# Input projection of a hybrid encoder layer: splitting the next weight tile before, instead of after, the next block's activations

## The reference

```python
xn = rmsnorm(xp, g_attn_pre[l])
h = xn @ w_in                                   # (tokens, 1024) @ (1024, 1184)
cq, ckv, kpe, qs, ks, vs = jnp.split(h, IN_SPLIT_POINTS, axis=-1)
q = (rmsnorm(cq, g_q) @ w_uq).reshape(b, t, MLA_HEADS, MLA_NOPE + MLA_ROPE)
ckv_n = rmsnorm(ckv, g_kv);  kpe = rope(kpe, pos)
```

## Time and profile before

| | us |
|---|---|
| median of three runs | 2798.33 |
| lowest and highest of them | 2790.84, 2800.78 |
| the profiled execution | 2798.33 |
| its span, first to last instruction | 2796.5 |
| TensorE busy in the span | 2672.3 (96%) |
| VectorE, ScalarE, GpSimd busy | 1900.8, 1425.9, 481.4 |

### The profile page before, as it was taken

How to read it: one execution, slowest core, us unless ns; L and a number is a source line. 1 busy time by engine, 2 the same in 40 slices (tenths; PEclk the granted TensorE clock), 3 DMA queues, 4 the chain that set the end, 5 groups by cost and what they waited for, 6 DMA issues and landing times.

```text
span 2796.5 us, 44995 instructions
## 1 busy us (share of the span) xinstructions
PE 2672.3 (96%) x13603; PEld 2439.9 (87%) x13603; DVE 1900.8 (68%) x2793; ACT 1425.9 (51%) x3042; POOL 481.4 (17%) x400
## 2 busy tenths in 40 slices
PE   8999978999999987999999999999999999999997
PEld 7999844677777776999999999999999999999997
DVE  6877677788788737777478754687546875568743
ACT  5443367576667744644355443454435544355532
POOL 1111041244334433000200022000220002200001
PEclk9999999899999999999999999999999999999999
DMA  7666655444555242343334433244333443334432
GB/s 220 215 216 230 218 146 154 81 76 84 88 87 86 71 140 76 113 135 122 114 99 138 163 117 109 96 140 161 116 113 102 136 163 117 104 103 131 127 119 88
DMA packets 181776, 357.73 MB, mean 128 GB/s; under 512 B 50693, under 2 KB 119781, under 8 KB 180325
## 3 DMA queue, kind: packets, MB, share of 16 engines
q1 hardware_dynamic: 181636, 356.00, 42.5%
HBM read 301.28 MB, written 55.43 MB: 128 GB/s over the span
## 4 chain that ended last, share of the span: by engine, by line
PE 56%; DVE 3%; ACT 1%; issue 1%; DMA 1%; POOL 1%; SPq 0%; ACTq 0%; DVEq 0%; POOLq 0%
PE mf_acc L2191 56%; DVE mix_w_lo L2352 1%; DMA room<-in_w_up 1%; ACT mix_w_hi L2245 1%; POOL mf_ss L2147 1%; PE mf_st L2229 0%; DMA room<-in_w_out 0%; DVE mf_x L2370 0%; DVE mf_x L2375 0%; DVE mf_rstd L2387 0%; DVE mf_xn L2403 0%; DVE mf_y L2457 0%; DVE mf_y L2465 0%; ACT mf_sq L2268 0%; ACT mf_sq L2302 0%
## 5 line engine op out<-in xcount | busy, mean ns | idle before, releaser
L2352 DVE TENSOR_TENSOR mix_w_lo<-room,mix_w_hi 128x1024 fp32r<-128x1024 f32 (+1 forms) x338 | 471.2, 1394 | 559.9 <-ACT mix_w_hi L2245 559.2
L2191 PE MATMUL mf_acc<-mix_a_hi,mix_w_hi 128*128 128x424 f32 (+1 forms) x2016 | 724.0, 359 | 30.1 <-ACTq L2248 12.2
L2191 PE MATMUL mf_acc<-mix_a_lo,mix_w_hi 128*128 128x424 f32 (+1 forms) x2016 | 717.3, 356 | 0.0
L2191 PE MATMUL mf_acc<-mix_a_hi,mix_w_lo 128*128 128x424 f32 (+1 forms) x2016 | 717.1, 356 | 0.0
L2245 ACT ACTIVATE mix_w_hi<-room 128x1024 fp32r<-128x1024 f32 (+1 forms) x338 | 383.1, 1133 | 520.8 <-PE mf_acc L2191 486.7
L2191 PEld LDWEIGHTS mf_acc<-mix_a_hi,mix_w_hi 128*128 128x128 f32 x2016 | 382.0, 189 | 45.7 <-issue 16.7
L2191 PEld LDWEIGHTS mf_acc<-mix_a_hi,mix_w_lo 128*128 128x128 f32 x2016 | 382.5, 190 | 10.5
L2191 PEld LDWEIGHTS mf_acc<-mix_a_lo,mix_w_hi 128*128 128x128 f32 x2016 | 382.2, 190 | 8.7 <-issue 0.7
L2191 PE MATMUL mf_acc<-mf_h_hi,mix_w_hi 128*128 128x424 f32 (+1 forms) x944 | 338.9, 359 | 6.9 <-DVE mix_w_lo L2352 3.9
L2191 PE MATMUL mf_acc<-mf_h_hi,mix_w_lo 128*128 128x424 f32 (+1 forms) x944 | 335.0, 355 | 0.0
L2191 PE MATMUL mf_acc<-mf_h_lo,mix_w_hi 128*128 128x424 f32 (+1 forms) x944 | 334.6, 354 | 0.0
(11 more groups left out here) (204 smaller groups left out, 4099.5 us busy)
## 6 DMA issues: line engine op xcount, KB each, us to landing
room<-in_w_up SPq DMA_DIRECT2D x220, 512.0 KB, 3.5
room<-in_w_down SPq DMA_DIRECT2D x80, 704.0 KB, 4.1
pi_w_raw<-in_w_in SPq DMA_DIRECT2D x49, 512.0 KB, 6.1
room<-in_w_out SPq DMA_DIRECT2D x40, 512.0 KB, 3.6
la_rec_all<-inv_scr SPq DMA_DIRECT2D x32, 256.0 KB
ahead_k<-kn_scr SPq DMA_DIRECT2D x28, 280.0 KB, 5.4
ahead_q<-qn_scr SPq DMA_DIRECT2D x28, 264.0 KB, 5.1
room<-in_x SPq DMA_DIRECT2D x4, 1696.0 KB, 12.0
```

Source lines behind the costliest of these rows:

```text
L2191: mm = pe.matmul(acc[:, t_bank[0], 0:n], w[:, g, k], x[:, k, 0:n], start=(first and k == 0 and m == 0), stop=(last and k == count - 1 and ...
L2352: dve.tensor_tensor(w_lo[:, g, 0:count], w_raw[:, g, 0:count], w_hi[:, g, 0:count].bitcast(F32), ALU.subtract).then_inc(w_split, 1)
```

## The change

At steps j = 4 to 9 ScalarE and VectorE used to make the x tile of the next block first and split the weight tile after it. At j = 2 and 3 it was the other way round. The change makes j = 4 to 9 like j = 2 and 3: weight tile first, x tile after it. No instruction is added or removed, and SyncE, GpSimd and TensorE keep their order.

```diff
@@ ScalarE @@
-                    if 4 <= j <= KD + 1 and not last:
-                        x_tile(b + 1, j - 2, 1 - par)
                     if t + SLOTS - 1 < TILES and t > 0:
                         w_hi_of(t + SLOTS - 1)
-                    if 2 <= j < 4 and not last:
+                    if 2 <= j <= KD + 1 and not last:
                         x_tile(b + 1, j - 2, 1 - par)
```

## The result

The changed kernel takes 2812.44 us (median of five runs, 2810.11 to 2814.5), the kernel before 2797.61 us beside it: a ratio of 1.0056 with a 95% interval of 1.004 to 1.0072. Measured a second time as e1_again it took 2808.3 us against 2798.66, 1.0041 (1.0025 to 1.0057). So it is slower by about 0.4 to 0.6%, some 10 to 15 us. I forecast 2805 with a range up to 2812, which the first median passes by 0.4 us, and gave slower by over 0.5% a chance of 0.09.

What follows compares the result with a forecast made beforehand. TensorE, busy 96% of the span, was taken as the bound; 4.7 us of boundary delay at tile 41 plus 1.7 for one clock fall made 6.4 us on 2798.33, forecast 2805 us, range 2795 to 2812.

Steps and rivals of the forecast that it cites:

- End of block 0: First block boundary: the x tile starts one weight tile later, so TensorE, already waiting for it, slips 1.1 us.
- End of block 1: Second boundary: weight tile 22 split 1.3 us late, TensorE waits 1.5 us for x tile 7, sum slips 2.6.
- the ring: Chain of VectorE, ScalarE and SyncE beside TensorE's own, product to store to x load; weight tiles 1.3 us late at boundaries.
- End of block 2: Third boundary: weight tile 32 split at 207.4, x tile 7 done at 210.3, sum at 210.85, slip 4.4 us.
- End of block 3: Fourth boundary: weight tile 42 at 272.2, sum at 275.65, slip 5.95; tile 41 at 278.65, +4.7 us.
- accumulator wait: TensorE's 1.06 us wait at 273.94, before tile 41, for a freed accumulator; forecast to vanish.
- Clock: TensorE's clock after new boundary waits of 1.5 to 1.9 us: one fall taken, +1.7 us, bounds 0 and 10.
- Inside a block: Steps j = 4 to 8: -0.6 us at j = 4 in blocks 2 and 3, +0.15 in block 1, otherwise nothing.
- Rival A: Block boundaries: TensorE drags the ring along, lateness repeats in full; +9.0 us, 2809 with one clock fall; chance 0.16.
- Rival B: Block boundaries: nothing moves, the last x tile turns out early enough; 2798 us; chance 0.10.
- C (long falls): Three boundary waits: each brings a clock fall, mean price 5.0 us, giving 2818 us; chance 0.09.
- D (faster): Projection: earlier weight splits bring the ring ahead, waits of 1.0 and 1.3 us go; 2796 us; chance 0.08.

Runs made afterwards that it cites:

- e3_last_only: Kernel before with only step j = 9 swapped, j = 4 to 8 as before: 2812.17 us, ratio 1.0044 (1.0029 to 1.0059).
- e4_add_waits: Changed kernel with GpSimd's addition of a block's last squares waiting until VectorE has made the last x tile: 2809.87 us, ratio 1.0037 to the kernel before.
- e7_tensor_late: Kernel before with eight extra sums on TensorE ahead of the sum at the start of block 2, delaying TensorE alone: 2802.0 us, one run.
- e2_last_old: Changed kernel with step j = 9 put back as before, so only j = 4 to 8 swapped: 2801.03 us, ratio 1.0008 (0.9999 to 1.0017).

## Why the prediction was wrong

What makes the loss, its place and its sign were right. How the loss is carried from one boundary to the next was not, and so the size was too small, 6.4 us for what is 9.8 us at tile 41 (both with one clock fall) and 9.6 and 14.8 us in the two measurements. Step by step:

- *End of block 0*, forecast 1.1: measured 2.4. VectorE's chain was already 1.3 us late when it reached the swapped pair (79.67 for 78.38). Of it, 0.5 is the store of `q_scr` (product at 68.16 for 67.62, which scatters), and 0.7 a latent's scaling that took 1.34 us for 0.66, beside an addition on GpSimd. The second part goes with the swaps of j = 4 to 8: the scaling took 0.81 to 1.55 us in the five traces that have them, 0.66 in the other five. The swap of the last step then cost the forecast 1.1.
- *End of block 1*, forecast ring 1.3 late and x tile 0.65 us long: measured 2.9 and 1.47. The slip at the sum is 5.1 for 2.6: my 2.6, plus 1.6 of a later ring, plus 0.8 of the x tile, make 5.0.
- *End of block 2*, forecast weight tile 32 at 207.4, slip 4.4. Measured 210.91 and 8.9. Again 4.4 + 3.5 + 0.8 = 8.7.
- *End of block 3*, forecast weight tile 42 at 272.2, slip 5.95. Measured 276.26 and 11.0, with 5.95 + 4.1 + 0.8 = 10.8; and tile 41 at 283.70, not 278.65. The accumulator wait went as forecast.
- *Clock*, forecast one fall at 1.7 us: there was one, behind the sum at 148.25, where the granted clock is 0.57 over 4 us (below), 1.7 us by the slip of later rows. It fell by luck on the forecast number: e1_again had one fall at another boundary, e3_last_only and e4_add_waits three.
- *Inside a block*, forecast -0.6 at j = 4 and nothing at j = 6 to 8: the idle 0.67 us of the earlier trace rows shrank to 0.25, but what was gained was lost at once, as the x tile behind it now takes 1.50 us:

```profile
179.24 1.23 DVE L544 TENSOR_TENSOR pi_w_lo<-pi_w_raw,pi_w_hi 128x1024 fp32r<-128x1024 f32 x1 [0.25 <-ACT pi_w_hi L412]
180.39 1.50 DVE L549 SCALAR_TENSOR_TENSOR pi_x_lo<-room,pi_gx,pi_x_hi 128x424 fp32r<-128x424 f32 x1
```

The step that failed is the lateness of the ring, which I took as 1.3 us at every boundary because steps of 65 us on one chain and 63.3 on the other looked like two clocks of their own. It was 2.9, 4.8 and 5.4 us. The chains are coupled: ScalarE and VectorE take the expansions from TensorE in order, between two weight splits, at j = 1 to 3 (e7). To measure it over all traces I take TensorE's lateness behind the boundary and its clock fall, at the last sum of the latents of a block:

```profile
184.48 0.87 PE L712 MATMUL pi_st<-pi_lat_sq,pi_ones 128*128 128x424 f32 x2
...
247.81 0.87 PE L712 MATMUL pi_st<-pi_lat_sq,pi_ones 128*128 128x424 f32 x2
```

Against these rows of before and the earlier trace rows, in us:

| execution | block 2: TensorE late | weight tile 32 late | difference | block 3: TensorE late | weight tile 42 late | difference |
|---|---|---|---|---|---|---|
| changed kernel | 6.75 | 4.84 | 1.91 | 8.92 | 5.36 | 3.56 |
| e1_again | 4.69 | 2.55 | 2.14 | 6.63 | 3.28 | 3.35 |
| e4_add_waits | 5.53 | 3.85 | 1.68 | 7.76 | 4.48 | 3.28 |
| e3_last_only | 5.64 | 3.86 | 1.78 | 9.54 | 7.38 | 2.16 |
| e7_tensor_late | 5.73 | 3.91 | 1.82 | 5.73 | 3.56 | 2.17 |

In block 2 the ring is late by what TensorE is late less 1.7 to 2.1 us, for delays of TensorE from 4.7 to 6.8 us: a slack, and beyond it TensorE's slip at one boundary is the ring's lateness at the next. In block 1 there is no slack: weight tile 22 is as late as TensorE (taken at 121.15 in the kernel before) or up to 0.6 us later in all seven traces in which it waits for its load. In block 3 the difference is 3.3 to 3.6 us where j = 4 to 8 are swapped as well, which is what a ring would show that by itself falls back another 1.7 us per block, but 2.2 in e3_last_only and e7_tensor_late. Why these two differ was not tried. The clock fall that I had added by itself is inside the lateness, since it delays TensorE like a wait.

Of the 5.1 us missed at tile 41 (9.8 less 4.7), 4.1 are the ring's lateness and 0.8 is the collision with GpSimd, which I had not priced for the x tile. The 4.1 is not made by the coupling: it is the 1.3 us more of block 0, the clock fall and the waits, which the coupling hands on from one boundary to the next. Rival A, at +9.0 us and a chance of 0.16, had the coupling and nearly the number, though without the slack: block 0 and the collision made up for that. What stands ahead of `w_hi` at j = 1 to 3 would have told me.

Rival B is excluded by both measurements, C (long falls) and D (faster) by the traces. The two measurements put the loss at 9.6 and 14.8 us; traces account for 9 to 10 in the projection of either. Whether the other 5 us of the first are scatter alone or lie elsewhere is left open; the intervals of the two ratios overlap. More clock falls at the boundaries are one candidate: each profiled execution of the changed kernel had one, e3_last_only and e4_add_waits had three. No trace shows how many the timed runs had.

## What to carry to other kernels

- An engine that executes in order hands on every wait ahead of it: before placing work of TensorE's next few microseconds behind a split that waits for a DMA, compare when each is needed, not how long each takes. Here one swapped step out of six cost 0.4% by itself (e3_last_only); the other five cost nothing that can be told (e2_last_old).
- Two chains with different periods in a profile are not independent if any instruction of one waits for the other once per round. Look for it before taking a lateness as constant; delaying one of them alone (e7) shows that they are coupled, and one more size of delay tells a slack from a chain of its own.
- A late load can be a matter of its place in the queue. Moving it ahead of two stores, at the same time of issue, made its split possible at least 4.7 us earlier; it gains only where somebody has come to need it.

## What the runs showed of the hardware

The low parts that VectorE makes, of an x tile (three operands) and of a weight tile (two), and GpSimd's addition of squares do not run side by side; whichever starts second waits for the other. The x tile takes 0.64 to 0.66 us alone. When it starts 0 to 0.1 us behind GpSimd's addition of 1.1 us it takes 1.46 to 1.56 us, and wherever it starts beside one it ends about 0.45 us behind it (146.04 + 1.47 against 145.93 + 1.13). In the projection of the kernel before, four x tiles took about 1.5 us and two 1.3; in the changed kernel sixteen took 1.46 to 1.56, since the weight tile ahead of it on VectorE now ends just as its squares are ready. The low part of a weight tile, 1.2 us alone, ends 1.08 or 1.09 us behind an addition that it starts beside; an addition that starts beside either low part ends 0.92 to 0.97 us behind that (all in the traces of these two kernels). Where the two starts stand within 0.02 us of each other, either can be the one that is held. Both ways, from the changed kernel and from the one before:

```profile
59.99 2.13 DVE L544 TENSOR_TENSOR pi_w_lo<-pi_w_raw,pi_w_hi 128x1024 fp32r<-128x1024 f32 x1
59.66 1.37 POOL L531 TENSOR_TENSOR pi_ss<-pi_sq,pi_ss 128x424 f32<-128x424 f32 x1 [2.27 <-ACT pi_sq L441]
```

```profile
47.02 1.22 DVE L546 TENSOR_TENSOR pi_w_lo<-pi_w_raw,pi_w_hi 128x1024 fp32r<-128x1024 f32 x1
47.07 2.12 POOL L533 TENSOR_TENSOR pi_ss<-pi_sq,pi_ss 128x424 f32<-128x424 f32 x1 [3.79 <-ACT pi_sq L441]
```

The reciprocal is not held: at 56.84 in the kernel before it takes its 2.80 us beside an addition that takes 1.10.

The clock fell behind some gaps of 1.8 to 3.2 us in a dense stretch and not behind others, of 1.6 to 2.3 us. TensorE's windows of the changed kernel, in the columns of the earlier trace rows, begin with one that fell to a mixture of 1.2 and 2.4 GHz, after 2.46 us of idling; after 1.91 us, at 214.67, it stayed at 2.4:

```profile
148.00:152.00 4.00, 4.00 (x13) 0.57 0.97 358
...
214.00:218.00 4.00, 3.33 (x15) 1.00 1.03 370
```

In e3_last_only it was the other way round: none after 2.31 us at 148.06, a fall after 2.04 us at 213.69. A single trace can't tell what such a wait costs in the mean: over the four traces with the last step swapped (after, e1, e3, e4) there were eight falls at sixteen boundaries. Two of them, in e4_add_waits, came behind a pair of shorter gaps (1.64 and 0.38, 1.28 and 0.71 us) with three matmuls between.
